# First scan of a two-block kernel: half of the chunks on crossed partition halves, and a turned inverse made by identity products

## The reference, cut to what matters

```
def step(state, inp):
    r_t, w_t, k_t, v_t, kk_t, a_t = inp
    sa = jnp.einsum('bhvk,bhk->bhv', state, -kk_t)
    state = (state * w_t[:, :, None, :]
             + sa[..., :, None] * (kk_t * a_t)[..., None, :]
             + v_t[..., :, None] * k_t[..., None, :])
    y = jnp.einsum('bhvk,bhk->bhv', state, r_t)
    return state, y
_, ys = lax.scan(step, state0, xs, reverse=reverse)
```

## Time and profile before

| what | value |
|---|---|
| median of 3 runs | 2623.36 us (2622.28 to 2632.97) |
| span of the profiled execution | 2624.7 us |
| PE busy in the whole span | 2274.1 us |
| rounds 1 to 7, from the first level to the last end product | 306.11 to 503.74 us |

### The profile page before, as it was taken

The page is one execution under the profiler, slowest core; times in us unless marked ns, Lnnn a source line. Parts: engine busy times, 40 slices in busy tenths (PEclk is TensorE's granted clock), DMA queues, the critical chain, the costliest instruction groups (busy, mean ns, idle before and its releaser), DMA issues. The chain is left out here.

```text
span 2624.7 us, 46494 instructions
## 1 busy us (share of the span) xinstructions
PE 2274.1 (87%) x17118; PEld 1290.6 (49%) x17118; DVE 1605.6 (61%) x3740; ACT 1152.0 (44%) x2884; POOL 998.5 (38%) x694
## 2 busy tenths in 40 slices
PE   7997999988988987777787877877789997899998
PEld 5774899866444432222232222222258765643334
DVE  6886666448777776666766667676558854520002
ACT  4547433336444444444444444444354234433434
POOL 0001211103544556666666765667700300133331
PEclk9998999999999999999999999999999999989999
DMA  8742100326999999999999999999957411489995
GB/s 340 291 159 72 40 20 20 122 75 270 417 412 414 415 419 421 421 422 421 421 421 407 422 417 416 407 419 420 416 198 254 157 46 66 166 338 372 365 359 200
DMA packets 161062, 778.07 MB, mean 296 GB/s; under 512 B 34610, under 2 KB 52674, under 8 KB 77379
## 3 DMA queue, kind: packets, MB, share of 16 engines
q0 software_dynamic: 87552, 545.34, 50.6%
q1 hardware_dynamic: 72274, 227.47, 23.0%
q10 hardware_dynamic: 1008, 2.29, 0.2%
HBM read 821.14 MB, written 18.88 MB: 320 GB/s over the span
## 5 line engine op out<-in xcount | busy, mean ns | idle before, releaser
L2599 PE MATMUL bank<-expert_rows,diagonals 128*128 128x512 f32 x1604 | 784.6, 615 | 189.3 <-ACT diagonals L2430 189.0
L2255 POOL DMA_INDIRECT expert_rows<-in_uv,expert_idx x426 | 656.1, 1540 | 423.7 <-PE bank L2599 165.0
L2312 DVE SCALAR_TENSOR_TENSOR expert_rows<-expert_rows,h_rows 128x1024 f32<-128x1024 f32 x426 | 522.0, 1225 | 320.8 <-DMA expert_rows<-in_uv,expert_idx 298.5
L2599 PEld LDWEIGHTS bank<-expert_rows,diagonals 128*128 128x128 f32 x1604 | 278.6, 190 | 650.3 <-ACT diagonals L2430 433.1
L2420 ACT ACTIVATE expert_act<-expert_dot 128x1 f32<-128x1 f32 x512 | 103.7, 203 | 674.2 <-DVE expert_rows L2312 557.0
L2430 ACT ACTIVATE diagonals<-ident,expert_weight 128x128 f32<-128x128 f32 x512 | 205.4, 401 | 16.7
L2599 PE MATMUL bank<-weight_slots,diagonals 128*128 128x512 f32 x344 | 170.6, 621 | 46.9 <-ACT diagonals L2430 46.6
L2255 POOL DMA_INDIRECT weight_slots<-in_uv,expert_idx x86 | 144.4, 1679 | 73.8 <-issue 39.2
L2426 ACT ACTIVATE expert_weight<-expert_act,expert_gate 128x1 f32<-128x1 f32 x512 | 150.8, 294 | 17.2
L3996 DVE TENSOR_TENSOR hidden<-hidden,bank 128x256 f32<-128x256 f32 x24 | 10.1, 421 | 239.8 <-ACT hidden L3853 239.8
L2312 DVE SCALAR_TENSOR_TENSOR weight_slots<-weight_slots,h_rows 128x1024 f32<-128x1024 f32 x86 | 105.5, 1227 | 68.4 <-DMA weight_slots<-in_uv,expert_idx 61.8
(11 more groups left out here) (627 smaller groups left out, 4013.9 us busy)
## 6 DMA issues: line engine op xcount, KB each, us to landing
expert_w<-in_experts SPq DMA_DIRECT2D x55, 1024.0 KB, 10.5
expert_w_more<-in_experts SPq DMA_DIRECT2D x41, 1024.0 KB, 9.9
x<-in_ada_rows SPq DMA_DIRECT2D x32, 512.0 KB, 5.3
weight_slots<-in_w_in SPq DMA_DIRECT2D x8, 1536.0 KB, 9.2
mod_rows<-in_ada_rows SPq DMA_DIRECT2D x11, 1024.0 KB, 6.5
mixed<-in_ada_rows SPq DMA_DIRECT2D x10, 1024.0 KB, 4.8
weight_slots<-in_w_in SPq DMA_DIRECT2D x4, 2048.0 KB, 9.9
weight_slots<-in_att_bias SPq DMA_DIRECT2D x8, 1024.0 KB, 6.9
```

Source lines behind the costliest of these rows:

```text
L2255: pool.indirect_dma_start(rows[j], None, core.dram["uv"], bass.IndirectOffsetOnAxis(idx[:, t, column:column + 1], 0)).then_inc(arrived[j], 16)
L2312: dve.scalar_tensor_tensor(out=u, in0=u, scalar=1.0, in1=hN[:, t % 2, :], op0=ALU.mult, op1=ALU.mult, accum_out=dot[:, j:j + 1]).then_inc( ...
L2599: mm = pe.matmul(bank[2 * (t % 2) + half][:, :], diag[:, j, :], rows[slot_of(n)][:, D + half * S:D + half * S + S], start=column == 0, sto ...
```

## The change

Chunks 4 to 7 (q = 1) move to crossed halves. Where an operand or a result of these chunks is not also needed with the others' layout, head 0 stands on partitions 64 to 127 and head 1 on 0 to 63; products read one layout and write the other, so chunk i of q = 0 and chunk i of q = 1 are issued back to back on the four quadrants, into two different PSUM banks. This holds for `turn` 1, grams 0 and 1, xs, all level products, and the end products for `ahat` and `y0`. Turns 0, 2, 3, grams 2 to 4, the gain product, the chain and the y products stay as they were. Gram 1 is made for chunks 0 to 3 only; chunks 4 to 7 of it are made with gram 0.

`w_products` is split. `inv_products` makes only the new columns of `inv`; `invT` comes from `turn_inverse`, a product of `inv` with the identity, issued behind the next level's `z_products`. In the last level `last_products` makes `invT` as before. Each of the two kinds now waits for both halves. Numbers of matmuls in a round: 8 more than before in gram 0 and 1, none elsewhere.

The chain of round n-1 is spread wider: no step behind turn 1 and grams 0 and 1; steps 8 to 13 in levels 0 to 2. `y_product` of one chunk at a time stands behind `z` and `inv` in levels 0 to 3. ACT's `scale_bonus` moves from level 1 to level 3. In round 0 `rate_units(OPENING)` moves behind all turns.

```
+    def both_halves(out, lhs, rhs, c, was=0, to=0):
+        for h in range(2):
+            mm = pe.matmul(out(h ^ to), chunk(lhs, c, h ^ was), rhs(h ^ was), start=True, stop=True)
+        return mm
+    def side_by_side(banks, lhs, rhs, was):
+        for i in range(HALF):
+            for q in range(2):
+                c = q * HALF + i
+                mm = both_halves(lambda h: chunk(banks[q], c, h), lhs, lambda h: chunk(rhs, c, h), c, was * q, (1 - was) * q)
+        return mm
...
+    def first_grams(n):
+        pe.wait_ge(turn_out, copy_no(n, 1))
+        for c in range(NC):
+            both_halves(lambda h: chunk(FAR, c, h), beta, lambda h: chunk(alpha, c, h), c)
+            if c < HALF:
+                d = c + HALF
+                mm = both_halves(lambda h: chunk(NEAR, d, h), beta, lambda h: chunk(alpha, d, h), d, 0, 1)
+            else:
+                mm = both_halves(lambda h: chunk(NEAR, c - HALF, h), alpha, lambda h: chunk(beta, c, h), c, 0, 1)
+        mm.then_inc(grams, 1)
+        for c in range(HALF):
+            mm = both_halves(lambda h: chunk(bank[GRAM_BANK[1]], c, h), alpha, lambda h: chunk(beta, c, h), c)
+        mm.then_inc(grams, 1)
...
+    def z_products(n, l):
+        was = inv0[n % 2] if l == 0 else inv
+        if l == 0:
+            pe.wait_ge(gram_out, GRAM_OUT(n, 4))
+        else:
+            pe.wait_ge(inv_out, INV_OUT(n, l - 1))
+        level_products(z_bank, 0, tri[n % 2], lambda c, j: chunk(was, c, j), RLEVELS[l], early_late(n)[0], 1, z_full)
+    def inv_products(n, l):
+        was_t, merged = invT0[n % 2] if l == 0 else invT, off[n % 2][l]
+        pe.wait_ge(z_out, 2 * NL * n + 2 * l + 2)
...
+        if l >= 1:
+            pe.wait_ge(tail_out, TAIL_OUT(n, l - 1))
+        level_products(w_bank, 0, was_t, lambda c, j: chunk(merged, c, j), RLEVELS[l], None if l == 0 else early_late(n)[0], 0, inv_full)
+    def turn_inverse(n, l):
+        pe.wait_ge(inv_out, INV_OUT(n, l))
+        level_products(w_bank, 4 * RC, inv, lambda c, j: eye_of(j), RLEVELS[l], None if l == 0 else early_late(n)[1], 1, tail_full)
...
 # order of a round on PE
+    first_grams(n)
+    for g in range(2, 5):
+        chain(n - 1, g + 1)
+        gram(n, g)
+    chain(n - 1, 6)
     xs_products(n)
+    chain(n - 1, 7)
     for l in range(NL):
         z_products(n, l)
+        if l >= 1:
+            turn_inverse(n, l - 1)
...
+        if l < 3:
+            chain(n - 1, 8 + 2 * l)
+        if l < NL - 1:
+            y_product(n - 1, 2 * l)
+            inv_products(n, l)
+            if l < 3:
+                chain(n - 1, 9 + 2 * l)
+            y_product(n - 1, 2 * l + 1)
         else:
+            last_products(n)
     end_products(n)
...
 # DVE, grams 0 and 1 in pieces
+    if g == 0:
+        pick(tri[n % 2][:, cols_of(0)], FAR[:, cols_of(0)], 0)
+        pick(tri[n % 2][:, cols_of(1)], NEAR[:, cols_of(1)], 0)
+        pick(inv0[n % 2][:, cols_of(1)], NEAR[:, cols_of(0)], 2)
+        pick(invT0[n % 2], FAR[:, :], 1)
+    elif g == 1:
+        pick(inv0[n % 2][:, cols_of(0)], bank[GRAM_BANK[1]][:, cols_of(0)], 2)
```

More of the change, by code:

```diff
@@ L1429, in gains @@
                     part = slice(1, NC) if rev_of(n) else slice(0, NC - 1)
-                    dve.tensor_tensor(units(gain)[:, part, :], units(bank[END_BANK[2]][:, :])[:, part, :], repeat(step[:, n % 2, 0:NC - 1], HD),
+                    dve.tensor_tensor(units(gain)[:, part, :], units(GAIN_BANK[:, :])[:, part, :], repeat(step[:, n % 2, 0:NC - 1], HD),
                                       ALU.mult).then_inc(gain_out, 1)
@@ new lines, in _ @@
+                            if l < NL - 1:
+                                act.wait_ge(inv_full, 2 * (NL - 1) * n + 2 * l + h + 1)
+                                if l == 0:
+                                    act.activation(inv[:, cols_of(h)], w_bank[h][:, 0:4 * RC], ACT.Copy).then_inc(inv_out, 1)
+                                else:
+                                    act.activation(columns(inv[:, cols_of(h)], m, early), compact(w_bank[h][:, 0:2 * RC], m), ACT.Copy).then_inc(inv_out, 1)
@@ L1685, in _ @@
                                 raise_unit(u)
[L1686 removed]
+                        if l == 3 and rev_of(n):
                             scale_bonus(pair_of(n))
@@ L1723, in turn @@
                         pe.wait_ge(ops_dve, 3 * n + j)
+                    if j == 1 and n == 0:
+                        pe.wait_ge(unit_raised, 4)
                     if n >= 1:
-                        if j == 2:
-                            pe.wait_ge(end_out, 2 * n)
-                        elif j == 3:
-                            pe.wait_ge(gain_out, n)
-                    for c in range(NC):
-                        for h in range(2):
-                            mm = pe.matmul(chunk(bank[TURN_BANK[j]], c, h), chunk(src, c, h), core.ident[half_rows(h), half_rows(h)], start=True, stop=True)
@@ L1732, in turn @@
-                    mm.then_inc(turned, 1)
+                        if j == 1:
+                            pe.wait_ge(end_out, 4 * n - 2)
+                        elif j == 2:
+                            pe.wait_ge(end_out, 4 * n)
+                    if j == 1:
+                        for i in range(HALF):
+                            for q, ps in enumerate((NEAR, FAR)):
+                                c = q * HALF + i
+                                mm = both_halves(lambda h: chunk(ps, c, h), src, eye_of, c, 0, q)
+                    else:
+                        for c in range(NC):
+                            mm = both_halves(lambda h: chunk(bank[TURN_BANK[j]], c, h), src, eye_of, c)
@@ L1741, in gram @@
                     for c in range(NC):
[L1742 to L1743 removed]
+                        mm = both_halves(lambda h: chunk(bank[GRAM_BANK[g]], c, h), lhs, lambda h: chunk(rhs, c, h), c)
                     mm.then_inc(grams, 1)
                 def xs_products(n):
[L1747 to L1748 removed]
@@ new lines, in xs_products, with level_products @@
+                    side_by_side((NEAR, FAR), ka, vN[pair_of(n) % 2], 0).then_inc(xs_full, 1)
+                def level_products(banks, at, lhs, moving, m, half, was, full):
+                    for i in range(HALF):
+                        for q in range(2):
+                            c = q * HALF + i
+                            if half is None:
+                                out = lambda j: chunk(banks[q][:, at:at + HALF * RC], i, j)
+                                rhs = lambda j: moving(c, j)
+                            else:
+                                out = lambda j: compact(banks[q][half_rows(j), at + i * RC // 2:at + (i + 1) * RC // 2], m)
+                                rhs = lambda j: columns(moving(c, j), m, half)
+                            mm = both_halves(out, lhs, rhs, c, was * q, (1 - was) * q)
+                            if i == HALF - 1:
+                                mm.then_inc(full, 1)
```

203 lines of the change are left out of this document (86 added, 117 removed).

## The result

The changed kernel takes 2643.14 us (median of 5 runs, 2642.28 to 2644.92), the kernel before 2628.88 beside it: a ratio of 1.0054 [1.0037, 1.0071]. It is 14 us slower where 2600 was forecast: a miss of 43 us. Some 4 us of these are the kernel before itself, whose median is 2628.88 here and whose span in the forecast was 2624.7; against the kernel before the miss is 39 us (25 less forecast, 14 more measured).

The account below looks back on a forecast made before the run. PE's pace through small products bounds the scan (busy 194.64 of 197.63 us). Savings of 15.4 + 1.2 (levels), 7.5 + 1.0 (passages), -0.5 (start), 0.8 (end) make 25.4 off 2624.7: 2599, stated as 2600; own range 2586 to 2612, over cases 2585 to 2629.

Parts of the forecast that it names:

- the sum: Whole kernel: savings in levels, passages and end, less a cost at the start, add to 25.4 us off 2624.7: 2599.
- the step to round 1: Passage from round 0 to round 1: 16.6 us before, unexplained PE idle left in, 1.0 us saved.
- rival C: PE idles a third of the levels; half-clock stretches cost about 1.7 us each, 15 undo the gain; chance 0.05.
- A quad is 0.117 us: Products on four quadrants: two of each half together take 0.117 us, the time of one two-product unit before.
- Rival B: Quadrants don't overlap: a quad costs 0.233 us, five levels some 20.5 us, the kernel 2651; chance 0.08.
- Five levels are 14.85 us: Levels 0 to 4 of a round, z0 to E: 14.85 us against 17.05 before.
- Between E and z0 11.4 and 12.3: Passage from levels to next round's: 11.4 us to an odd round (12.83 before), 12.3 to an even one (13.35).
- PE idles 4 to 5 us a round, ended by turned copies: In the levels PE waits 4 to 5 us a round, until ACT has copied the turned products.
- Levels of round 0 16.5, to round 1 15.6: First round's levels fall from 17.73 to 16.5 us; the following passage, 16.6 before, saves 1.0.
- Clock 1.00: Granted clock in the profile after stays 1.00; stretches at half clock in the scan would make the forecast wrong.
- Rival A: Latency eats it: split waits cost 0.5 us more a level, 1 us a passage; 2620 to 2628; chance 0.15.
- D: More comes through: y products and chain fill less, copies overlap better; 40 us saved, 2584; chance 0.07.

Follow-up runs that it names:

- quad burst: Changed kernel plus 256 quads, then 256 pairs of unread products behind the scan's end: 2725.3 us in one run; the quads took 55.8 us.
- half by half run: Changed kernel with each product group issued for chunks 0 to 3, then 4 to 7, with a wait for each half: 2634.3 us, ratio 1.0025.
- after: The changed kernel itself, against the kernel before: 2643.1 us, ratio 1.0054.
- shift: Changed kernel with 32 small products (128 instructions) added ahead of round 0: 2629.4 us, ratio 1.0017 to the kernel before.
- fill: Changed kernel with unread one-quadrant products around the levels' inverse and last products in rounds 1 to 7: 2634.0 us, ratio 1.0025 to the kernel before.
- fill and shift: Changed kernel with both the unread filler products and 32 small products ahead of round 0: 2639.3 us, ratio 1.0044 to the kernel before.
- two with less y: Changed kernel with two of y's three products left out, without fillers (2631.9 us, 1.0009) and with fillers (2634.1 us, 1.0014).
- quarter run: Changed kernel with 55 pairs a round (grams 2 to 4, gain, y) replaced by 14 of 256 columns, results partly wrong: 2617.0 us, ratio 0.9953.
- its control: Kernel before with the same 55 pairs a round replaced by 14 pairs of 256 columns: 2623.4 us, ratio 0.9988.

## Why the prediction was wrong

**The step that failed** is *the sum*, by a term that isn't in it. PE's end was worked out from what it has to do (units, quads) and what it has to wait for (masks, copies). What it takes to bring PE its instructions was in no term. The sign of it stood in the rows: the step to round 1 has "an idle of PE with nothing to wait for", and I left it in as an oddity of that place. It was a block coming late: its packet starts 8 us after the one before it and 2.4 us before PE goes on.

The arithmetic could have been done. From z0 of round 1 to E of round 7 the changed kernel issues 6641 matmuls and as many loads, 51.9 blocks; at 3.47 us each that is 180 us. The forecast for this stretch is 197.63 - 15.4 - 7.5 = 174.7. So it asked for blocks faster (3.37 us) than they come. In the kernel before 51.1 blocks stand in 197.63 us, 3.87 us each, and a pair eats a block in 3.73: PE's own pace just hid the supply. In the changed kernel the mean alone would cost 5 us. The rest comes from single blocks that are late. A quad burst eats one in 1.88 us and leaves less time for the next; but most of the stop time follows packets that came more than 4.5 us after their predecessor, and the half by half run has as many stops without quads. What delays these packets stays open, but for the coincidence with the 1 and 2 MB transfers.

**The clock** (rival C, 0.05) was named with the right mechanism and too small a chance. "With PE at two thirds I am between the two, nearer the second" looked at means: the stops make single stretches far emptier than the mean, and the clock fell behind stretches of 1.5 to 2.11 us of 3.40 busy, though not behind all such. The price was too high: over 42 rounds of six kernels (after, shift, fill, fill and shift, and two with less y) a least-squares fit gives 27.9 us a round + 0.96 for each us of stops + 0.28 for each us at half clock, that is 0.95 us for a stretch of 3.4 and not 1.7. The clock and the stops aren't independent: the quarter run has fewer stops and less time at half clock too (0.96 for 0.89).

How the miss divides, as far as runs show it: the supply some 23 (quarter less its control), the clock 8 to 15 (fill), and these overlap where a stop brings half clock, so they don't simply add up. The fit gives an estimate of the same: the seven rounds, 32.97 us in the mean for 27.2 forecast (190.7 us from gain to gain, with the step to round 1), are 40 us over, of which 18 go with stops, 16 with the half clock and 4 with neither. The mean round of the quarter run, 28.67 us, still stands 1.4 us over the forecast, with 7.6 us of stops and 9 us at half clock left in these rounds. What an undisturbed changed kernel would take wasn't measured: no version here is free of both.

**Point by point.**
- *A quad is 0.117 us*: right (0.67 us for 16 products, 0.117 in the burst). Rival B fell as it was put, while a long burst does pay 0.218, for want of instructions. The rule of the Trainium skill that the prediction cites against its value ("TensorE: Matmul & The Clock Gate", section "The mechanism" of part 3) would have given nearly the right time for that burst, 0.233 us a quad, for a wrong reason. Within a block a quad took 0.117 us, so there the loads of two tiles on one row group did not queue.
- *Five levels are 14.85 us*: right within 0.5 where nothing disturbs it (15.30); 16.94 in round 3 with two stops.
- *Between E and z0 11.4 and 12.3*: the mechanism was right (waits for L1426 and L1430, 0.4 us each), 11.47 in the quarter run; 14.03 and 15.22 at clocks of 0.82 and 0.80.
- *PE idles 4 to 5 us a round, ended by turned copies*: all idle time was 42 us in 6.6 rounds, 6.4 a round; turned and last copies took 2.1 of it and stops another 2.5.
- *Levels of round 0 16.5, to round 1 15.6*: 18.68 and 16.90, at clocks of 0.81 and 0.80.
- *Clock 1.00*: wrong, 0.88.
- *Rival A* (longer hand-overs): at most 0.6 us a round by the fit, where it has 3.5; *D*: not seen, and at a block each 3.47 us it would be out of reach.

## What to carry to other kernels

When a change makes PE work through many small instructions faster, count them: matmuls and loads divided by 256, times the spacing of the instruction queue's packets in your own trace (3.47 us here), is a bound for every long stretch. It isn't the whole price: in this scan it accounts for 5 us, and the stops took 20. A stop with nothing to wait for in the trace of before is the sign to look for; see whether a packet of the instruction queue starts a short time before its end (2.2 to 2.9 us here), and what else moves data then. Making the same products on more quadrants lowers PE's time but not that count; fewer and wider instructions lower both. And where a change lets PE idle that was busy before, give the clock a real chance, and price it by a run with fillers.

## What the runs showed of the hardware that was not expected

- PE's instructions come in blocks of 256, in a burst one each 3.47 us; four quadrants with 64-column fp32 products eat one in 1.88 us, two quadrants in 3.73.
- Each of the 21 stops of PE without a semaphore between 306 and 520 us ends 2.2 to 2.9 us after a packet of the instruction queue starts; the longest follow packets that came 5.8 and 7.9 us after the one before, beside a transfer of 1 or 2 MB on another queue.
- Adding 128 instructions ahead of the scan made the changed kernel 10 us faster, mostly by the clock (0.94 for 0.89), and gave nothing with fillers.
- A pair of fp32 products costs 0.117 us for 32 or 64 columns and 0.433 for 256: from 64 to 32 columns the price doesn't fall.
- 5 us more work of PE in 240 brought the granted clock from 0.89 to 0.99.
